# Chosen distances between the split buffers, and the late modulation rows of the first stage moved, in a four-layer transformer kernel on one core

## The reference

```python
def modulation(c, w, b):   # w: 1024 x 3072 per sublayer
    return jnp.split(jax.nn.silu(c) @ w + b, 3, axis=-1)
def sandwich(x, mod, g_pre, g_post, fn):
    shift, scale, gate = mod
    h = rms_norm(x, g_pre) * (1.0 + scale[:, None]) + shift[:, None]
    return x + gate[:, None] * rms_norm(fn(h), g_post)
for layer in range(2):
    # layer 0: pooling + HGRN2 ("hyb"), layer 1: dilated attention ("att")
    x = sandwich(x, modulation(c, ada_w[layer, 0], ada_b[layer, 0]), norm_pre[layer, 0], norm_post[layer, 0], mixer)
    x = sandwich(x, modulation(c, ada_w[layer, 1], ada_b[layer, 1]), norm_pre[layer, 1], norm_post[layer, 1], ffn)
for layer in range(2):
    # layer 0: forgetting attention + S5 ("fox"), layer 1: mLSTM ("mls")
    h = layer_norm(DN_ALPHA * h + mix, ln_g[layer, 0], ln_b[layer, 0])
    ffn = hier_moe(h, ...)          # 4 groups x 4 experts, top 2
    h = layer_norm(DN_ALPHA * h + ffn, ln_g[layer, 1], ln_b[layer, 1])
```

## Time and profile before

| | us |
|---|---|
| median of 3 runs | 1543.95 |
| lowest, highest | 1541.48, 1548.09 |
| profiled execution, its own time | 1546.48 |
| its span (first to last instruction) | 1544.6 |

### The profile page before, as it was taken

One profiled execution on the slowest core, in us unless ns is written; L12 is line 12 of the kernel. 1 busy time (PEld: TensorE's weight loads), 2 busy tenths in 40 slices (PEclk: granted clock), 3 DMA queues, 4 the chain that ended last, 5 costly groups with the idle time before them and its releaser, 6 DMA issues.

```text
span 1544.6 us, 25597 instructions
## 1 busy us (share of the span) xinstructions
PE 1459.0 (94%) x10156; PEld 1336.0 (86%) x10156; DVE 1153.7 (75%) x1737; ACT 812.9 (53%) x1177; POOL 1.2 (0%) x5
## 2 busy tenths in 40 slices
PE   7988999999999999999999799999989999999996
PEld 7877799999998979999978678899979987898995
DVE  4887876875856656697478977889969754888995
ACT  1431433434443345535575437887745554677773
POOL 0000000000000000000000000000000000000000
PEclk8889999999999999999999999999999999999998
DMA  9882689986565515565633135999924542689990
GB/s 376 297 301 71 218 300 323 339 289 205 192 204 165 164 42 178 176 190 179 188 104 122 69 125 207 357 343 379 333 66 139 165 136 69 211 333 350 340 368 34
DMA packets 184202, 333.94 MB, mean 216 GB/s; under 512 B 13308, under 2 KB 127508, under 8 KB 184084
## 3 DMA queue, kind: packets, MB, share of 16 engines
q1 hardware_dynamic: 184084, 332.31, 63.0%
HBM read 331.18 MB, written 1.09 MB: 215 GB/s over the span
## 4 chain that ended last, share of the span: by engine, by line
PE 75%; DVE 11%; ACT 3%; issue 3%; DMA 1%; ACTq 0%; DVEq 0%
PE PSA L604 15%; PE PSA L606 15%; PE PSA L605 15%; PE PSA L601 9%; PE PSB L604 6%; PE PSB L606 6%; PE PSB L605 6%; PE PSB L601 2%; DVE WL L1804 2%; DVE T L1804 2%; ACT WH L1327 1%; DMA WR<-ffn_w_in 1%; DVE AR L1804 1%; DVE ACC L1801 1%; ACT T L1317 1%
## 5 line engine op out<-in xcount | busy, mean ns | idle before, releaser
L1804 DVE TENSOR_TENSOR WL<-WR,WH 128x1024 fp32r<-128x1024 f32 x352 | 421.3, 1219 | 134.7 <-ACT WH L1327 134.3
L1327 ACT CAST WH<-WR 128x1024 fp32r<-128x1024 f32 x352 | 354.9, 1048 | 109.5 <-DMA WR<-hyb_w_in 42.5
L604 PE MATMUL PSA<-XH,WH 128*128 128x256 f32 x1312 | 378.0, 288 | 6.8 <-DVE AR L2188 2.5
L606 PE MATMUL PSA<-XH,WL 128*128 128x256 f32 x1312 | 373.2, 284 | 0.0
L605 PE MATMUL PSA<-XL,WH 128*128 128x256 f32 x1312 | 372.6, 284 | 0.0
L604 PEld LDWEIGHTS PSA<-XH,WH 128*128 128x128 f32 x1312 | 250.6, 191 | 11.1 <-issue 2.8
L605 PEld LDWEIGHTS PSA<-XL,WH 128*128 128x128 f32 x1312 | 251.0, 191 | 1.1 <-issue 0.5
L606 PEld LDWEIGHTS PSA<-XH,WL 128*128 128x128 f32 x1312 | 249.8, 190 | 0.0
L1804 DVE TENSOR_TENSOR WL<-AR,WH 128x1024 fp32r<-128x1024 f32 x152 | 178.3, 1219 | 22.1 <-ACT WH L1327 22.1
L604 PE MATMUL PSB<-WH,GH 128*128 128x512 f32 x448 | 179.7, 401 | 3.0 <-DVE GL L1804 3.0
L606 PE MATMUL PSB<-WH,GL 128*128 128x512 f32 x448 | 177.6, 396 | 0.0
(11 more groups left out here) (260 smaller groups left out, 2250.4 us busy)
## 6 DMA issues: line engine op xcount, KB each, us to landing
WR<-ffn_w_in SPq DMA_DIRECT2D x88, 512.0 KB, 4.6
AR<-ada_w SPq DMA_DIRECT2D x58, 512.0 KB, 8.2
AR<-moe_w_down SPq DMA_DIRECT2D x56, 512.0 KB, 6.4
AR<-moe_w_gate SPq DMA_DIRECT2D x48, 512.0 KB, 6.1
AR<-moe_w_up SPq DMA_DIRECT2D x48, 512.0 KB, 6.2
WR<-ffn_w_out SPq DMA_DIRECT2D x44, 512.0 KB, 4.6
WR<-att_w_qkv SPq DMA_DIRECT2D x36, 512.0 KB, 5.0
AD<-ada_w SPq DMA_DIRECT2D x34, 512.0 KB, 5.8
```

The lines of the kernel that those rows point to most:

```text
L604: e.matmul(o, lh, rh, start=start, stop=False, skip_group_check=True)
L606: return e.matmul(o, ll, rh, start=False, stop=stop, skip_group_check=True)
L1327: A(e.copy(hi_slot(m), raw_slot(m)), s_hi)
L1804: return e.tensor_tensor(o, i, j, op)
```

## The change

It has two parts.

**Distances.** The tensors are declared in another order, with three unused gaps of 16, 16 and 24 numbers, and SM is 48 numbers shorter. Placed so: XH 24704, T1/T1R 32896, XL 41152, WH 49408, GH 69888, WL 78848, GL 99328, T2/T2R 119808, WR 132096, ARR/AR 148480. XH to XL is now 16448 bytes (was 8192), WH to WL and GH to GL 29440 (were 20480 and 8192). All of these begin at a multiple of 64; XL alone is not a multiple of 128.

**Late rows.** Parts 3 and 4 change places: the gate of sublayer 0 comes before the shift of sublayer 1. The steps are put behind other pieces, four of them (32 to 35) behind the levels. Two slabs get places of their own. The gate's total goes to banks 4 and 5 (`gring`) ahead of `down`.

```diff
-ADA_PARTS = [(0, 1), (0, 0), (1, 1), (1, 0), (0, 2), (2, 1), (2, 0), (1, 2), (3, 1), (3, 0), (2, 2), (3, 2)]
+ADA_PARTS = [(0, 1), (0, 0), (1, 1), (0, 2), (1, 0), (2, 1), (2, 0), (1, 2), (3, 1), (3, 0), (2, 2), (3, 2)]
+ADA_BEHIND_LEVELS = (32, 33, 34, 35)
...
-        offsets = (0, 1, 2, 2, 3, 3, 4, 4) if p == 3 else [k // rate for k in range(8)]
+        pieces = {3: (12, 12, 13, 13, 16, 17, 17, 18), 4: (22, 22, 22, 22, 23, 24, 25, 26)}.get(p, range(at, at + 8))
...
+            if 8 * p + k not in ADA_BEHIND_LEVELS:
+                step.setdefault(pieces[k], []).append(8 * p + k)
...
         XH = sb("XH", 2048, F32R)
+        T1R = rounded("T1R", 2048)
+        T1 = sb("T1", 2048)
+        sb("GAP0", 16)
         XL = sb("XL", 2048, F32R)
+        sb("GAP1", 16)
+        WH = sb("WH", NSPLIT * 1024, F32R)
         GHF = plain("GHF", 2048)
         GH = sb("GH", 2048, F32R)
+        MC = sb("MC", 168)
+        sb("GAP2", 24)
+        WL = sb("WL", NSPLIT * 1024, F32R)
         GLF = plain("GLF", 2048)
         GL = sb("GL", 2048, F32R)
...
+        gring = Ring(4, [sig(f"s_bank{i}_filled").sem for i in (4, 5)], [sig(f"s_bank{i}_free").sem for i in (4, 5)])
+
+        def ada_ring(p):
+            return pring if p < 2 else gring if p == 3 else ring
...
             t.then_inc(u.fill[0], 1)
+            e.wait_ge(*gring.uses["ada", 3].free)
             down(0, 1, True, False)
...
                         V.frees(e.copy_predicated(dst, rep(mask, 4), v3(bank(u.b), 4)), u)
+            ada_end(3)
+            for x in ADA_BEHIND_LEVELS:
+                ada_step(x)
             ss, o = ring.uses["ss"], ring.uses["o"]
```

More of the change, by code:

```diff
@@ L153, in ada_plan @@
     at = 1
-    for p, rate in ((2, 1), (3, 2), (4, 2), (5, 1), (6, 1), (7, 1), (8, 1), (9, 1), (10, 1), (11, 1)):
+    for p in range(2, 12):
         n, part = ADA_PARTS[p]
@@ L159, in ada_plan @@
             at = FIRST["att"] + 2
-        offsets = (0, 1, 2, 2, 3, 3, 4, 4) if p == 3 else [k // rate for k in range(8)]
+        pieces = {3: (12, 12, 13, 13, 16, 17, 17, 18), 4: (22, 22, 22, 22, 23, 24, 25, 26)}.get(p, range(at, at + 8))
         for k in range(8):
-            step.setdefault(at + offsets[k], []).append(8 * p + k)
-        last = at + offsets[7]
-        if part == 2:
+            if 8 * p + k not in ADA_BEHIND_LEVELS:
+                step.setdefault(pieces[k], []).append(8 * p + k)
+        last = pieces[7]
+        if part == 2 and p != 3:
             last = max(last, FIRST[STAGES[n]] + ROWS_LOADED + 8)
         total[last + 1] = p
-        end[last + (3 if p < 5 else 4)] = p
+        if p != 3:
+            end[last + (3 if p < 5 else 4)] = p
         at = last + (4 if p < 5 else 5)
@@ L189, in ada_places @@
     piece = {x: n for n, xs in ADA_STEP.items() for x in xs}
+    piece.update((x, 22) for x in ADA_BEHIND_LEVELS)
     place, count, before, load = [], [], [], {}
@@ L196, in ada_places @@
             i = (0, 1, 11, 12, 17, 16, 15, 11)[x - 16]
+        elif x < 32:
+            i = (0, 1, 16, 15, 18, 19, 20, 21)[x % 8]
         elif x < 40:
-            i = (0, 1, 16, 15, 18, 19, 20, 21)[x % 8]
+            i = (0, 1, 18, 28, 29, 19, 20, 21)[x % 8]
         elif x < 80:
@@ L207, in ada_places @@
         if x >= 20:
-            early = piece[x] - (9 if 24 <= x < 28 else 3 if 28 <= x < 32 else 6)
-            if i >= 22:
+            early = piece[x] - (9 if 24 <= x < 28 else 3 if 28 <= x < 32 else 8 if 32 <= x < 40 else 6)
+            if 22 <= i < 28:
                 early = max(early, FIRST["ffn", 0])
@@ L370, in build @@
         AD = sb("AD", 2048)
-        T1R = rounded("T1R", 2048)
-        T1 = sb("T1", 2048)
         T2R = rounded("T2R", 2048)
@@ L375, in build @@
         RS = sb("RS", 1024)
-        MC = sb("MC", 168)
-        SM = sb("SM", 800)
+        WR = sb("WR", NRAW * 1024)
+        ARR = rounded("ARR", ARENA)
+        AR = sb("AR", ARENA)
+        SM = sb("SM", 752)
         CT = sb("CT", CN)
         PR = sb("PR", PN)
[L380 to L384, removed]
         scratch = nc.dram_tensor("bias_rows", [24, 384], F32, kind="Internal")
@@ L390, in build @@
         s_raw = [sig(f"s_raw{i}_landed") for i in range(NRAW + NFAR)]
-        s_ada = [sig(f"s_ada{i}_landed") for i in range(28)]
+        s_ada = [sig(f"s_ada{i}_landed") for i in range(30)]
         s_hi, s_lo, s_used = sig("s_hi_made"), sig("s_lo_made"), sig("s_piece_used")
@@ L482, in build @@
         ada_at += [AR[:, x:x + 1024] for x in range(7168, 13312, 1024)]
+        ada_at += [AR[:, x:x + 1024] for x in (0, 5376)]
         accs = (ACC[:, :], AR[:, 1024:2048])
@@ L625, in ada_total @@
                 acc = accs[p == 1]
-                u = use(("ada", p), 2 if part == 2 else 1, of=pring if p == 0 else ring)
+                u = use(("ada", p), 2 if part == 2 else 1, of=ada_ring(p))
                 e.wait_ge(s_adastep.sem, ada_count(8 * p + 7))
@@ L1847, in ada_end @@
                 n, part = ADA_PARTS[p]
-                u = (pring if p < 2 else ring).uses["ada", p]
+                u = ada_ring(p).uses["ada", p]
                 filled(u)
@@ L1852, in ada_end @@
                     V.wait()
-                    V.frees(tt(RS[:, :], PSA[:, u.b * 512:u.b * 512 + 1024], RS[:, :], ALU.add), u)
+                    ps, o = (PSA if u.b < 4 else PSB), u.b % 4 * 512
+                    V.frees(tt(RS[:, :], ps[:, o:o + 1024], RS[:, :], ALU.add), u)
                     V.wait()
@@ L2724, in load_ada @@
                     e.wait_ge(s_adastep.sem, ada_count(ADA_BEFORE[x]))
-                elif 18 <= i < 22:
+                elif 18 <= i < 22 or i == 28:
                     e.wait_ge(s_dif.sem, 1)
+                elif i == 29:
+                    e.wait_ge(s_gh.sem, 1)
                 elif i >= 22:
```

## The result

| | before | changed |
|---|---|---|
| median of 10 runs each, us | 1548.05 | 1533.76 |
| lowest, highest | 1541.48, 1553.11 | 1530.26, 1540.79 |
| profiled execution, its span | 1546.48, 1544.6 | 1534.18, 1532.2 |

The ratio is 0.9916 with a 95% interval from 0.9894 to 0.9938: 0.84% faster, 13 to 14 us. The sign was right, and the forecast gain was three times the measured one; 1534 lies within the stated range (1488 to 1540).

The account below looks back on a forecast made before the run. TensorE, busy 94% of the span, was taken as the bound, with split matmuls 63% of the chain. From 1546.5 us, 36 for distances and 7 for moved rows left 1503.5, given as 1502 for the median; range 1488 to 1540.

Parts of the forecast that it names:

- Term A: Split matmuls on TensorE: new operand distances shorten pitches to 113.3 and 226.5 ns; 49 us of TensorE time, 36 us booked.
- places of operands cause the stall: Split streams on TensorE: operand addresses, not other engines, make the 8.5 ns between 226.5 and 235.0 ns with 512 columns.
- discount for hiding: Of 49 us on split matmuls, 36 reach the time: 6 of 13 in the MoE stages, 30 of 36 outside.
- Term B: First stage: moved modulation rows let level 2 start near 97.5 and the downs end near 166.5; 7 us, bounds 2 and 9.
- the added wait: First stage: `down(0)` waits for banks 4 and 5 until the gate's sum is read; forecast with 3.9 us of slack.
- placement without effect: Rival on split streams: the 8.5 ns come from another tensor's content or precision form, not its address; 1537 us, chance 0.20.
- Only half of the stall goes: Rival on split streams: pitch also depends on something besides the 32 bytes, so 18 us gained there; 1519 us, chance 0.20.
- Aligned operands meet: Rival on split streams: reads of congruent moving and stationary operands collide and pitches rise, 27 us; 1564 us, chance 0.05.

Follow-up runs that it names:

- all level: Changed kernel with the split buffers side by side and no gap, all beginning at the same place modulo 256; median 1537.67 us, ratio to before 0.9948.
- G level: Changed kernel with XH, XL, T1 side by side, a 64-byte gap before WH, WL, and GH, GL behind WL, level with the weights; 1527.91 us, ratio to before 0.9870.
- The streams alone: Three programs, kernel's work left out, TensorE running only split-product streams at varied operand places; best pitches 113.3 ns (256 columns) and 226.7 ns (512); no kernel time.
- weights 64 off: Changed kernel with XH, XL, T1, GH, GL side by side and WH, WL behind one 64-byte gap; median 1516.51 us, ratio to before 0.9808.
- rows alone: Changed kernel with the old tensor declarations, so only the modulation rows moved against the kernel before; median 1540.74 us, ratio to before 0.9950.

## Why the prediction was wrong

- **The bound** was read rightly: TensorE, and in it the split matmuls. Time followed the pitches in three kernels: 8.0 us less pitch gave 7.6 us alone, 17.2 gave some 17, and "all level" with 4.4 more took 4 to 5 more. "G level" shows that the granted clock can add to it as much as the pitches do.
- **Term A failed at its first line:** "I take the good stream's price for all: 226.5 ns for 512 columns, half of it, 113.3 ns, for 256." For the 1344 wide matmuls this was near (228.3 instead of 226.7; 7.7 of the 10.3 us). For the 6528 narrow ones it was worth nothing: 3936 x 0.0 for X moving, and -2.1, +1.2 and +0.5 us for W moving over XH/XL, GH/GL and T1R, a gain of 0.4 us where 26.4 + 12.4 = 38.8 were booked. The earlier trace rows showed one relation of places, for one width, in one tensor. The step from "the 32 bytes matter" to "a multiple of 64 is enough, whatever the width" had no row behind it. That XL lies 64 bytes off the others was known from the change and was given no price in the sum. Its count of the MoE stages was also off, without weight: 1920 of the 2592 stand there, not 1750, which is 0.8 us at 4.8 ns each.
- The reasoning that **places of operands cause the stall** was right. The streams alone show it with everything else idle. The Trainium skill's rule (page "TensorE: Matmul & The Clock Gate", section "Step-by-step: what each phase is for": moving operand and weights come through two independent ports) does not agree, if it is taken to mean that no placement changes a pitch: 113.3 and 120.0 ns differ by nothing but places. What it is that collides is not shown.
- **The discount for hiding** (36 of 49) does not show as a whole: 7.6 of 8.0 us arrived, in a measurement with some 2.5 us either way. In the MoE stages little was there to arrive: from the 6000th to the 7500th matmul, all within the first of them, it took 228.1 us before, 227.1 changed and 227.3 with the weights 64 off, where the pitches had 1.3 and 2.1 us less. So the half that was taken off there is neither shown right nor wrong.
- **Term B was right in size**, 7 us against 7.6 measured alone: level 2 10.5 us behind level 0, level 3 held up by 3.15 us, no stall ahead of the first row pieces, where the added wait stands. That `cross` and the 34 passes came so near to their forecast times owes 3.3 us to the earlier start of the levels. Two details were not foreseen. The half clock went to level 3 (3.78 us for 16 passes), so the 2 us that were to be regained at level 2 were in part lost there. And within the row pieces TensorE now waits for GL: 2.14 us in the changed kernel, 0.35 with the rows alone, between 0.37 and 2.07 in the six other kernels with the moved rows, and not at all in the two without them.
- **The rivals:** the time came closest to "placement without effect" (1537), but for another reason: the places had an effect on every kind of stream, and most of it fell out at zero or nearly cancelled. "Only half of the stall goes" (1519) had the reason that was right, that a pitch depends on more than the 32 bytes, and a size that was not. "Aligned operands meet" was given 0.05 and is half true: level operands do cost 120.0 with 256 columns, the slowest but a few. It does not decide, because before cost nearly as much: 119.9 with X moving and some 118 with W moving.

## What to carry to other kernels

One pair of streams shows that a property matters, not which value of it is good: before a price measured at one width and one distance is put on thousands of other instructions, run the streams themselves at their real distances, alone. Read the pitch in several stretches of the trace, since a mean can hide two patterns of which one is free to have. And where an engine is the bound for 94% of the span, the sum of its pitches is a measure that tells 1 us apart where single times scatter by 5, as long as the granted clock is read beside it.

## What the runs showed of the hardware

- The pitch of a stream of split matmuls depends on where its operands lie modulo 256 bytes (of a partition): 113.3 to 122.9 ns with 256 columns, 226.7 to 236.7 with 512. In units of 2.4 GHz cycles the best are 272 and 544, which is 17/16 of the columns.
- One set of places can hold two patterns (113.3 and 117.8; 117.8 and 121.3), and a stream keeps its pattern over many pieces (in "weights 64 off" X moving had a mean of 117.8 from 160 to 200 us and of 113.5 from 200 to 240). What selects it beyond "how it was entered" stays open, and so does the mechanism behind the patterns.
- Executions of one kernel differ by 5 to 10 us, and the granted clock with them: of the ten of the changed kernel the fastest (1530.26) had a mean of 0.986, the slowest (1540.79) 0.977. Two profiled executions with the same pitches, before and rows alone, and that of the changed kernel differ in the first 50 us: granted clock 0.76 and level 0 at 87.01 before, 0.80 and 88.14 with the rows alone, 0.83 and 83.67 changed. Over all ten kernels level 0 began between 83.38 and 89.53 us, so a single profile's event times in the first stage are good to 3 us, no better, and are best counted from one another.
